# One ring block for both compressions' weights, and three modulation rides that change place, in a 4-layer hybrid attention stack

## The chip, the core and the metric

The kernel runs on one core of one Trainium2 chip. Its time is the device time of one launch in microseconds (us). The profile is of one execution of the same program.

## The reference, cut to what matters

A sequence of 512 tokens of width 1024 (float32) goes through an AB layer, a CD layer and then four adaptive layers, whose gains, shifts and gates come from a modulation vector. The change lies in the CD layer, in the output projection ahead of it, and in the first adaptive layer:

```python
def layer_ab(x, ...):
    ...
    return x + mix @ w_out                       # the output projection ahead of the CD layer

def nsa_compress(z, pe, w1, w2):                 # once for keys, once for values
    ...
    return jax.nn.silu(flat @ w1) @ w2           # w1: (32*64, 128)

def layer_cd(x, ...):
    y = rms_norm(x, norm_g) @ w_in
    qc, kc, vc, ks, vs, kw, vw, gc, zc, cq, ckv, kr, zd = split_cols(y, CD_SPLITS)
    ...

ml = ada_mods(c, ada_w[i], ada_b[i])             # a vector by a 1024 x 6144 matrix, 6 chunks of 1024
mc = ada_mods(c_ctx, ada_w[i], ada_b[i])
hl = modulate(rms_norm_2(x, norm1_g[i]), ml[0], ml[1])
yc, yl = gqa_mixer(hl, hc, ang, at_w_qkv[occ], ...)   # joint attention over x and context
```

## The kernel before, in words

The program is written by hand for each engine. Activations stay on the chip (`X`, `H` and an arena). All weights pass through a **ring of three slots** of 4096 floats for each of 128 partitions. A load fills one slot ("a block", up to 2 MB) and SyncE (SP) issues the loads in the order in which the blocks are used: L1305 waits until the block three places earlier is free, L1308 issues the load's pieces. Because SP works in order, a load also waits for all loads ahead of it. `freed_by` (L1182 on) says what frees a block: for a block of projection weights the last tile that reads it, for a modulation block the end of its sums on VectorE (DVE), for a compression block the `misc_pe` count after its matmuls.

A `project` stage is a list of groups `(block, tiles, ride)`. For each tile TensorE (PE) runs the matmuls (L1407), ScalarE (ACT) or DVE takes the result out of its bank, and `t.after` lists side steps that each engine does behind that tile: `mean` (L1436), `spread` (L1448) and `swap` (L1465) on PE, the reciprocal (L2418), the scaling (L2430) and the rotation (L2444, L2448) on DVE, the cosine product on GpSimd (POOL, L2790). A tile's bank is reused 3 or 6 tiles later.

A **ride** is one of the 12 modulation blocks of a layer (8 chunks of 128 rows by 512 columns). Behind the last tile of its group, DVE waits for its load and adds the 8 chunks up, scaled by the condition, into `partial` (L2292 and L2296, 16 operations where both x and the context need them). PE's part is a "modulation": 8 products with a column of ones, into bank 7 (L1367); it is done only when the next group ends (`ride` pops what is pending), and waits for DVE's sums. DVE then adds the bias (L2279).

```
            def ride(a):

                if pending:
                    modulation(pending.pop())
                if a:
                    pending.append(a)
```

The stages that matter: `residual_halves` for `ab_out` (4 groups of 4 tiles of 256 columns; the group with the ride is cut behind its second tile, L471 to L475); the CD projections (`cd_groups`, L748 to L771; tiles 0 to 41 are numbered in their order, `after(34, ...)` names the 34th); CD attention; `cd_out`; the norm; the three joint projections `at_qkv` (L999 to L1008); joint attention; `at_o`.

Order of the ring's blocks, from ab_out to at_o (m = a modulation block; the numbers are columns of cd_in):

```
ab_out0 m ab_out1 | 1024 m 0 m uq ukv m 2048 m m 512 m cmpK cmpV 1536 2464 m | cd_out0 m cd_out1 | at0 at1 at2 | at_o0 m at_o1
```

`cmpK` and `cmpV` are the first compression weights for keys and for values, 1 MB each in two pieces (two halves of the partitions). 1536 is the block of the gates `Z2[:, 1..4]` (tiles 34 to 37), 512 the block of tiles 30 to 33. PE's `compress` of keys (L1544) comes behind tile 34, that of values behind tile 35.

Of the kernel before, what the change touches and what calls it, by code (L numbers as in the profile page):

```python
# [27 lines left out]
HD = 64  # L28
# [8 lines left out]
CMP_STRIDE, CMP_LEN, CMP_HID = 16, 32, 128  # L37
CMP_HALF = CMP_LEN // 2
NCMP = S // CMP_STRIDE - 1
# [205 lines left out]
def build_program(nc, dram, out_dram, stages_kept=10000):  # L245
    ctx = ExitStack()
    with ctx:
# [3 lines left out]
        def sem(name):  # L251
            return ctx.enter_context(nc.semaphore(name))
# [31 lines left out]
        def bank(b, n=BANK, at=0):  # L284
            return psum[:, b * BANK + at:b * BANK + at + n]
# [46 lines left out]
        misc_pe, misc_act, misc_dve = sem("misc_pe"), sem("misc_act"), sem("misc_dve")  # L332
# [10 lines left out]
        def block(view, upper=None):  # L343


            shape = view.shape
            n = 1
            for d in shape[1:]:
                n *= d
            k = shape[1] if len(shape) == 3 else 1  # L350
            pieces = [(lambda x: x[0:shape[0]].rearrange("p (k n) -> p k n", k=k) if len(shape) == 3 else x[0:shape[0]], view)]
            if upper is not None:
                pieces.append((lambda x: x[HD:2 * HD].rearrange("p (k n) -> p k n", k=k), upper))
            return block_of(n, pieces)

        def block_of(n, pieces):


            assert n <= SLOT, n
            blocks.append((n, pieces))  # L360
            return len(blocks) - 1

        def columns(k, n, *pieces):


            return block_of(k * n, [(lambda x, c0=c0, c1=c0 + src.shape[1]: x.rearrange("p (k n) -> p k n", k=k)[:, :, c0:c1],
                                     src.rearrange("(k p) n -> p k n", p=P)) for c0, src in pieces])

        def slot(b, k):

            return ring[:, b % RING, 0:blocks[b][0]].rearrange("p (k n) -> p k n", k=k)
# [11 lines left out]
        def next_ada():  # L383

            if not ada_left:
                return None
            layer, j = ada_left.pop(0)
            b = block(dram["ada_w"][layer, :, 512 * j:512 * j + 512].rearrange("(k p) n -> p k n", p=P))
            return b, layer, j

        def stage(kind, **kw):
            kw["kind"] = kind
            kw.setdefault("loads", [])
            stages.append(kw)
            return kw
# [21 lines left out]
        def t_tile(b, k, col, width, act, n, taker, op, dst, arg=None, part=0, tile=None):  # L417

            w = slot(b, k)
            return Tile([(w[:, i, col:col + width], act[:, i, 0:n]) for i in range(k)],  # L420
                        (part, width, n), taker, op, dst, arg, tile)
# [26 lines left out]
        def residual_halves(src, op, arg, normed, rides=0, **kw):  # L448


            bs, groups = [], []
            for i in range(2):
                bs.append(block(src[:, BANK * i:BANK * i + BANK].rearrange("(k p) n -> p k n", p=P)))
                if i < rides:
                    groups.append(next_ada())
            rode = groups + [None] * (4 - len(groups))
            groups = []
            for h, cs in enumerate(halves):
                for i in range(2):
                    tiles = []  # L460
                    for j in range(4):
                        k = 4 * i + j
                        t = t_tile(bs[i], KD, P * j, P, H[:, :, cs], HALF, "dve", op, X[:, k, cs], arg(k))
                        t.part = h
                        t.after = normed.squares(h, [k])
                        normed.made[h, k] = t
                        tiles.append(t)
                    groups.append((bs[i], tiles, rode[2 * h + i]))
            groups[2][1][1].after.append(("nsum", normed, 0))
            groups[2][1][2].after.append(("nspread", normed, 0))  # L470
            sums_tile, parts = groups[3][1][2], []  # L471
            for b, tiles, a in groups:

                parts += [(b, tiles[0:2], a), (b, tiles[2:], None)] if a else [(b, tiles, None)]
            return stage("project", groups=parts, sums_tile=sums_tile, **kw)  # L475

        def second_half(tiles, normed, sum_at, spread_at):

# [48 lines left out]
        for c0 in range(0, 2560, 512):  # L527
            b = block(dram["ab_in"][:, IDX_COLS + c0:IDX_COLS + c0 + 512].rearrange("(k p) n -> p k n", p=P))
# [180 lines left out]
        cd_groups, cd_list, cmp_freed = [], [], {}  # L709

        def cd_block(c0, c1):
            return block(dram["cd_in"][:, c0:c1].rearrange("(k p) n -> p k n", p=P))

        def cd_group(b, tiles, rides=False):
            cd_groups.append((b, tiles, next_ada() if rides else None))
            cd_list.extend(tiles)


        b = cd_block(1024, 1536)
        lat_z = [("copy", CQ[:, 0]), ("copy", CQ[:, 1]), ("copy", CKV[:, 0]), ("silu", Z2[:, 0])]  # L720
        tiles = [t_tile(b, KD, P * j, P, H[:, :, cs], HALF, "act", op, dst[:, cs]) for cs in halves
                 for j, (op, dst) in enumerate(lat_z)]
# [5 lines left out]
        b = cd_block(0, 512)  # L728
        tiles = [t_tile(b, KD, P * j, P, H, S, "act", "copy", QC[:, j]) for j in range(4)]
# [3 lines left out]
        pieces = []  # L733
        for i in range(2):
# [3 lines left out]
            for q in range(2):  # L738
                for g in range(2):
# [3 lines left out]
        b = block_of(2 * 768, pieces)  # L743
        tiles = [t_tile(b, 2, P * t, P, CQ, S, "act", "copy", QU[:, t] if t < 4 else QR[:, t - 4]) for t in range(6)]
        cd_group(b, tiles)
        b = block(dram["ukv"])
        w = ring[:, b % RING, 0:1024]
        tiles = [Tile([(w[:, P * t:P * t + P], CKV[:, 0, :])], (0, P, S), "act", "copy", KU[:, t]) for t in range(4)]  # L748
        tiles += [Tile([(CKV[:, 0, tt * P:tt * P + P], w[:, 512:1024])], (0, P, 512), "act", "copy", VD[:, tt, :])
                  for tt in range(ST)]  # L750
        cd_group(b, tiles, True)
        b = columns(KD, 512, (0, dram["cd_in"][:, 2048:2432]),
                    *((384 + ROT * i, dram["cd_in"][:, 2432:2464]) for i in range(4)))
        cd_group(b, [t_tile(b, KD, 384, P, H, S, "act", "copy", KR[:, 0]),
# [1 line left out]
        cd_group(b, [t_tile(b, KD, P * j, P, H, S, "act", "silu", Z2[:, 5 + j]) for j in (1, 2)], True)  # L756
        b = cd_block(512, 1024)
        tiles = [t_tile(b, KD, P * j, P, H, S, "act", "copy", dst[:, 0]) for j, dst in enumerate((KC, VC, KS, KW))]
        cd_group(b, tiles, True)
        for kv in range(2):  # L760
            b = block(dram["cmp_w1"][kv, 0:CMP_HALF * HD].rearrange("(l d) m -> d l m", d=HD),
                      dram["cmp_w1"][kv, CMP_HALF * HD:].rearrange("(l d) m -> d l m", d=HD))
            cmp_freed[b] = (misc_pe, 3 + kv)
            cd_group(b, [])
        cmp_blocks = list(cmp_freed)
        b = cd_block(1536, 2048)
        tiles = [t_tile(b, KD, P * j, P, H, S, "act", "silu", Z2[:, 1 + j]) for j in range(4)]
        cd_group(b, tiles)
        b = cd_block(2464, 2744)
        cd_group(b, [n_tile(b, KD, 24, 256, H, tt, "act", "copy", VSW[:, tt, :]) for tt in range(ST)], True)  # L770
        cd_group(b, [n_tile(b, KD, 0, 24, H, tt, "act", "sigmoid", GC[:, tt, :]) for tt in range(ST)])  # L771
# [223 lines left out]
        at_groups, at_list = [], []  # L995
        for c0 in range(0, 1536, 512):
            b = block(dram["at_qkv"][:, c0:c0 + 512].rearrange("(k p) n -> p k n", p=P))
            if c0 < 1024:
                tiles = [t_tile(b, KD, P * j, P, H, S, "act", "copy", Q[:, c0 // P + j]) for j in range(4)]  # L999
                tiles += [t_tile(b, KD, P * j, P, CH, C, "act", "copy", QX[:, c0 // P + j]) for j in range(4)]  # L1000
            else:
                tiles = [t_tile(b, KD, P * j, P, H, S, "act", "copy", K2[:, j, 0:S]) for j in range(2)]
                tiles += [t_tile(b, KD, P * j, P, CH, C, "act", "copy", K2[:, j, S:S + C]) for j in range(2)]
                for tt in range(6):
                    src, t0 = (H, tt) if tt < ST else (CH, tt - ST)
                    tiles.append(n_tile(b, KD, 256, 256, src, t0, "act", "copy", V2[:, tt, :]))
            at_groups.append((b, tiles, None))
            at_list += tiles  # L1008
        at_rope = (rope_t[:, 2 * S:2 * S + P], rope_t[:, 0:S], rope_t[:, S:2 * S], work)
        for t0, count, is_x in ((0, 4, True), (4, 4, False), (8, 4, True), (12, 4, False), (16, 2, True), (18, 2, False)):  # L1010
# [336 lines left out]
        def _(pe):  # L1347
# [8 lines left out]
            def weights(b):  # L1356
                pe.wait_ge(weights_in[b % RING], landed[b])
# [179 lines left out]

            def compress(_, v):

                b1 = cmp_blocks[v]  # L1540
                weights(b1)
                open_bank(6 + v)
                for l in range(CMP_HALF):
                    last = nc.tensor.matmul(bank(6 + v, 2 * NCMP), slot(b1, CMP_HALF)[:, l, :],  # L1544
                                            cmp_in[v][:, 2 * NCMP * l:2 * NCMP * (l + 1)], start=(l == 0),
                                            stop=(l == CMP_HALF - 1))
                last.then_inc(misc_pe, 1)
                bank_freed[6 + v] = (misc_act, v + 1)
# [1341 lines left out]
```

## Time and profile before

| | |
|---|---|
| median of 3 runs | 4087.72 us (4080.39 to 4090.18) |
| the profiled execution | 4087.81 us |
| its span | 4085.7 us |
| granted TensorE clock, mean | 0.978 |
| busy: PE, DVE, ACT, POOL | 3926.6, 1751.1, 932.8, 506.3 us |
| HBM read | 334.01 MB, 83 GB/s over the span |

The profiled execution's time is 2.1 us above its span. Times in rows are us from the span's start. In a timeline, one row is a merged run of like instructions: start, us, engine, line, operation, output <- input, shapes, count, and in brackets the idle time before it and what ended it. PEclk 1.00 is the upper level of TensorE's clock (2.4 GHz), 0.50 the lower (1.2 GHz). CD attention runs from 661 to 824 us of the span.

### The profile page before, as it was taken

How to read it: one execution, taken by the hardware profiler on the slowest of the kernel's cores; microseconds unless marked ns; L12 is line 12 of the kernel's file. 1: busy time of each engine (PE TensorE's matmuls, PEld its weight loads, DVE VectorE, ACT ScalarE, POOL GpSimd, SP SyncE). 2: the span in 40 equal slices, each digit the busy share in tenths (PEclk: the TensorE clock that was granted, in tenths of full speed). 3: DMA queues.
4: the chain of work that ended last, by engine and by line, in shares of the span. 5: the costliest groups of instructions: out<-in, count | busy, mean ns of one | idle time of the engine just before them, and what ended most of it. 6: DMA issues, size and time to landing. Idle time of an engine off the chain costs nothing.

```text
span 4085.7 us, 42004 instructions
## 1 busy us (share of the span) xinstructions
PE 3926.6 (96%) x16600; PEld 2671.4 (65%) x16604; DVE 1751.1 (43%) x3123; ACT 932.8 (23%) x2131; POOL 506.3 (12%) x414
## 2 busy tenths in 40 slices
PE   9999979999999999999999899999999999999997
PEld 4458436545655565656545578888558888678886
DVE  2654444732673223111010555654675665224343
ACT  1141213621452211100010442020312111212020
POOL 1000000000000000000000421112432121111121
PEclk8999989999999999999999999999999999999999
DMA  3112332021002123223121314443202444112221
GB/s 125 62 42 84 116 98 79 1 74 41 24 1 61 62 82 107 100 99 108 62 72 64 86 30 154 165 167 103 83 21 83 165 165 144 67 62 83 83 83 42
DMA packets 226770, 342.38 MB, mean 84 GB/s; under 512 B 32209, under 2 KB 100209, under 8 KB 226545
## 3 DMA queue, kind: packets, MB, share of 16 engines
q1 hardware_dynamic: 202064, 322.44, 23.0%
q0 software_dynamic: 6816, 10.01, 1.2%
q10 hardware_dynamic: 17696, 7.26, 0.7%
q8 instruction: 134, 2.20, 0.2%
q14 instruction: 60, 0.48, 0.0%
HBM read 334.01 MB, written 4.06 MB: 83 GB/s over the span
## 4 chain that ended last, share of the span: by engine, by line
PE 73%; DVE 3%; POOL 1%; ACT 1%; issue 1%; DMA 0%; DVEq 0%; ACTq 0%; POOLq 0%
PE psum L1638 28%; PE psum L1407 28%; PE psum L1591 5%; PE psum L1595 3%; PE psum L1762 2%; PE psum L1709 2%; PE psum L1739 1%; PE psum L1507 1%; POOL arena L2774 1%; PE psum L1367 1%; DVE small L2594 1%; ACT arena L2079 1%; DVE psum L2590 0%; DVE arena L2609 0%; PE psum L1665 0%
## 5 line engine op out<-in xcount | busy, mean ns | idle before, releaser
L1407 PE MATMUL psum<-H,ring 128*128 128x512 f32 (+1 forms) x3248 | 1160.5, 517 | 38.1 <-DMA ring<-in_cd_in 22.8
L1407 PEld LDWEIGHTS psum<-H,ring 128*128 128x128 f32 x3248 | 622.0, 193 | 554.8 <-issue 483.9
L1638 PE MATMUL psum<-arena,ring 128*128 128x256 f32 x1536 | 342.8, 380 | 2.8 <-ACT arena L1876 2.8
L2296 DVE SCALAR_TENSOR_TENSOR arena<-ring,cond,arena 128x512 f32<-128x512 f32 x448 | 320.5, 754 | 8.0
L1638 PEld LDWEIGHTS psum<-arena,ring 128*128 128x128 f32 x1536 | 290.4, 190 | 44.0 <-ACT arena L1876 5.3
L2731 POOL TENSOR_TENSOR ring<-ring 128x1024 f32<-128x1024 f32 x48 | 159.6, 3325 | 791.0 <-DVE arena L2143 791.0
L1638 PE MATMUL psum<-arena 128*128 128x256 f32 x1152 | 256.3, 379 | 0.4
L1638 PEld LDWEIGHTS psum<-arena 128*128 128x128 f32 x1152 | 218.6, 190 | 30.3 <-ACT arena L1881 0.7
L2594 DVE TENSOR_REDUCE small<-psum 128x1 f32<-128x512 f32 (+7 forms) x352 | 187.0, 566 | 116.8 <-PE psum L1721 51.6
L2279 DVE TENSOR_TENSOR mods<-psum,vec 128x4 f32<-128x4 f32 (+1 forms) x48 | 7.7, 161 | 509.1 <-PE psum L1367 508.2
L1591 PE MATMUL psum<-arena,ring 128*128 128x512 f32 x512 | 225.6, 593 | 0.2 <-issue 0.2
L2067 ACT ACTIVATE arena<-psum,small 128x256 f32<-128x256 f32 (+7 forms) x320 | 183.8, 579 | 121.7 <-DVE small L2594 79.5
L1407 PE MATMUL psum<-CH,ring 128*128 128x256 f32 x928 | 206.7, 380 | 0.0
L1407 PEld LDWEIGHTS psum<-CH,ring 128*128 128x128 f32 x928 | 175.2, 190 | 39.9 <-issue 14.3
L1739 PE MATMUL psum<-ident,arena 128*128 128x128 f32 x984 | 153.3, 286 | 33.4 <-ACT arena L2079 21.6
L1638 PE MATMUL psum<-H,ring 128*128 128x256 f32 x768 | 177.0, 383 | 5.2 <-issue 4.5
L1638 PE MATMUL psum<-CX,arena 128*128 128x256 f32 x768 | 175.0, 382 | 5.8 <-DVE CX L2163 5.8
L1831 ACT ACTIVATE arena<-psum 128x512 f32<-128x512 f32 (+1 forms) x116 | 61.1, 528 | 494.9 <-PE psum L1407 490.9
L1638 PE MATMUL psum<-CH,ring 128*128 128x256 f32 x768 | 169.7, 379 | 0.0
L1591 PEld LDWEIGHTS psum<-arena,ring 128*128 128x128 f32 x512 | 96.7, 190 | 108.6 <-issue 107.4
L1638 PEld LDWEIGHTS psum<-CX,arena 128*128 128x128 f32 x768 | 146.9, 192 | 27.1 <-issue 6.9
L1638 PEld LDWEIGHTS psum<-H,ring 128*128 128x128 f32 x768 | 145.7, 192 | 25.5 <-issue 5.2
(230 smaller groups left out, 4612.2 us busy)
## 6 DMA issues: line engine op xcount, KB each, us to landing
ring<-in_mlp_w SPq DMA_DIRECT2D x64, 2048.0 KB, 8.8
ring<-in_ada_w SPq DMA_DIRECT2D x48, 2048.0 KB, 7.9
ring<-in_na_qkv SPq DMA_DIRECT2D x6, 2048.0 KB, 8.0
ring<-in_ab_in SPq DMA_DIRECT2D x5, 2048.0 KB, 8.2
ring<-in_cd_in SPq DMA_DIRECT2D x4, 2048.0 KB, 7.7
ring<-in_pw SPq DMA_DIRECT2D x8, 1024.0 KB, 6.8
ring<-in_at_qkv SPq DMA_DIRECT2D x3, 2048.0 KB, 7.8
ring<-in_ab_out SPq DMA_DIRECT2D x2, 2048.0 KB, 8.2
```

What stands on the lines that cost most here:

```text
L1407: last = nc.tensor.matmul(out, lhs, rhs, start=(k == 0), stop=(k == len(t.pairs) - 1))
L1591: last = nc.tensor.matmul(bank(m), w[:, k, P * m:P * m + P], hid[:, KD * kb + k, :], start=(kb == 0 and k == 0), stop=(kb == 3 and k == KD ...
L1595: last = nc.tensor.matmul(bank(4 + m // 2, C, C * (m % 2)), w[:, k, P * m:P * m + P], hidc[:, KD * kb + k, :], start=(kb == 0 and k == 0 a ...
L1638: last = nc.tensor.matmul(bank(at, HALF, HALF * m), w[:, i, P * m:P * m + P], x[:, i, :], start=(opens and m == 0 and i == 0), stop=(i == ...
L1709: last = nc.tensor.matmul(psum[:, at:at + k1 - k0], p["q"](g, qt * P, qt * P + P), p["k"](g, a * P + k0, a * P + k1), start=(m < 3), stop= ...
L1739: last = nc.tensor.transpose(psum[0:rows, c0:c0 + P], pair["probs"][g][:, k0:k0 + rows], ident[:, :])
L1762: last = nc.tensor.matmul(psum[HD * g:HD * g + HD, at + q0:at + q1], p["v"](g, of[0] if of else kt), chunk["turned"][0:p["krows"], kt, g, ...
L1831: nc.scalar.activation(t.dst, src, ACT.Copy).then_inc(act_took, 1)
L2067: nc.scalar.activation(pair["probs"][g][:, 0:nk + more], psum[:, off:off + nk + more], ACT.Exp, bias=small[:, c:c + 1], accum_out=small[:, ...
L2296: ins = nc.vector.scalar_tensor_tensor(partial[:, v, :], w[:, k, :], cond[:, k, v:v + 1], partial[:, v, :], ALU.mult, ALU.add)
L2594: nc.vector.tensor_reduce(small[:, c:c + 1], psum[:, off:off + nk], AX, ALU.max, negate=True).then_inc(negmax_ready, 1)
L2731: nc.gpsimd.tensor_tensor(a21, a11, a21, ALU.subtract).then_inc(s3_made, 1)
```

## The change

`residual_halves` no longer cuts the group with the ride: the ride comes behind the group's fourth tile, and PE's modulation one group later. In the CD projections, the groups of `ukv` and of block 512 carry no ride any more; `cmpK` and `cmpV` are one block of 4096 floats per partition in four pieces, freed by the fourth `misc_pe` (behind both compressions); the group of block 1536 is cut behind its first tile and carries a ride there. The second joint projection (`at_qkv` columns 512 to 1023) carries a ride. So six rides instead of seven lie in the CD projections and one in the joint projections; their number in all is the same. The ring's order becomes:

```
ab_out0 m ab_out1 | 1024 m 0 m uq ukv 2048 m m 512 cmp 1536 m 2464 m | cd_out0 m cd_out1 | at0 at1 m at2 | at_o0 m at_o1
```

```diff
-            sums_tile, parts = groups[3][1][2], []
-            for b, tiles, a in groups:
-
-                parts += [(b, tiles[0:2], a), (b, tiles[2:], None)] if a else [(b, tiles, None)]
-            return stage("project", groups=parts, sums_tile=sums_tile, **kw)
+            return stage("project", groups=groups, sums_tile=groups[3][1][2], **kw)
...
-        cd_group(b, tiles, True)
+        cd_group(b, tiles)
         b = columns(KD, 512, (0, dram["cd_in"][:, 2048:2432]),
...
-        cd_group(b, tiles, True)
+        cd_group(b, tiles)
+
+        pieces = []
         for kv in range(2):
-            b = block(dram["cmp_w1"][kv, 0:CMP_HALF * HD].rearrange("(l d) m -> d l m", d=HD),
-                      dram["cmp_w1"][kv, CMP_HALF * HD:].rearrange("(l d) m -> d l m", d=HD))
-            cmp_freed[b] = (misc_pe, 3 + kv)
-            cd_group(b, [])
-        cmp_blocks = list(cmp_freed)
+            for half in range(2):
+                pieces.append((lambda x, kv=kv, lo=HD * half: x[lo:lo + HD].rearrange(
+                                   "p (v l m) -> p v l m", v=2, m=CMP_HID)[:, kv],
+                               dram["cmp_w1"][kv, CMP_HALF * HD * half:CMP_HALF * HD * half + CMP_HALF * HD].rearrange(
+                                   "(l d) m -> d l m", d=HD)))
+        cmp_block = block_of(2 * CMP_HALF * CMP_HID, pieces)
+        cmp_freed[cmp_block] = (misc_pe, 4)
+        cd_group(cmp_block, [])
         b = cd_block(1536, 2048)
         tiles = [t_tile(b, KD, P * j, P, H, S, "act", "silu", Z2[:, 1 + j]) for j in range(4)]
-        cd_group(b, tiles)
+        cd_group(b, tiles[0:1], True)
+        cd_group(b, tiles[1:])
...
-            at_groups.append((b, tiles, None))
+            at_groups.append((b, tiles, next_ada() if c0 == 512 else None))
...
-                b1 = cmp_blocks[v]
-                weights(b1)
+                weights(cmp_block)
                 open_bank(6 + v)
                 for l in range(CMP_HALF):
-                    last = nc.tensor.matmul(bank(6 + v, 2 * NCMP), slot(b1, CMP_HALF)[:, l, :],
+                    last = nc.tensor.matmul(bank(6 + v, 2 * NCMP), slot(cmp_block, 2 * CMP_HALF)[:, CMP_HALF * v + l, :],
```

## Rows read from the trace of the kernel before

**Rows 1.** PE's waits over the span: us in total, times, longest us.
```profile
PE psum L1407 <- DMA ring<-in_cd_in: 22.8, 2, 18.0
...
PE psum L1367 <- DVE arena L2296: 4.1, 1, 4.1
```
**Rows 2.** Timeline of PE in ab_out.
```profile
320.87 14.05 PE L1407 MATMUL psum<-H,ring 128*128 128x256 f32 x64 [1.03 <-issue]
339.06 2.57 PE L1367 MATMUL psum<-ones,arena 128*128 128x1 f32 x16 [4.14 <-DVE arena L2296]
341.50 23.68 PE L1407 MATMUL psum<-H,ring 128*128 128x256 f32 x96
...
369.35 20.88 PE L1407 MATMUL psum<-H,ring 128*128 128x256 f32 x96
```
**Rows 3.** Timeline of DVE in ab_out.
```profile
329.18 9.83 DVE L2296 SCALAR_TENSOR_TENSOR arena<-ring,cond,arena 128x512 f32<-128x512 f32 x14
```
**Rows 4.** Stretch behind the first wait: us, busy by engine, PEclk, DMA, GB/s.
```profile
341.50:345.00 3.50, 3.50 (x9) 2.84 (x10) 0.17 (x1) 0.00 (x0) 0.00 (x0) 0.50 0.00 0
```
**Rows 5.** Timeline of PE in the CD projections.
```profile
502.35 1.95 PE L1367 MATMUL psum<-ones,arena 128*128 128x1 f32 x16
...
527.20 16.04 PE L1407 MATMUL psum<-H,ring 128*128 128x512 f32 x32 [4.87 <-DMA ring<-in_cd_in]
...
544.23 7.13 PE L1407 MATMUL psum<-H,ring 128*128 128x512 f32 x16
...
566.06 1.92 PE L1367 MATMUL psum<-ones,arena 128*128 128x1 f32 x16 [0.93 <-DVE arena L2444]
585.96 8.81 PE L1407 MATMUL psum<-H,ring 128*128 128x512 f32 x16 [17.98 <-DMA ring<-in_cd_in]
```
**Rows 6.** Timeline of SP in the CD projections: the issues of loads.
```profile
519.43 0.37 SPq L1308 DMA_DIRECT2D ring<-in_cd_in  x1
...
536.04 29.57 SPq L1308 DMA_DIRECT2D ring<-in_cmp_w  x4
578.28 21.61 SPq L1308 DMA_DIRECT2D ring<-in_cd_in  x2
```
**Rows 7.** Timeline of DVE: two modulation blocks' sums, and the reciprocal behind tile 34.
```profile
526.66 9.36 DVE L2296 SCALAR_TENSOR_TENSOR arena<-ring,cond,arena 128x512 f32<-128x512 f32 x14
...
568.90 9.36 DVE L2296 SCALAR_TENSOR_TENSOR arena<-ring,cond,arena 128x512 f32<-128x512 f32 x14
597.43 3.35 DVE L2418 RECIPROCAL arena<-arena 128x512 f32<-128x512 f32 x1 [19.18 <-ACT arena L1967]
```
**Rows 8.** DMA issues from 519 to 537: KB each, median us to landing.
```profile
ring<-in_cd_in SPq DMA_DIRECT2D x1, 2048.0 KB, 7.7
...
ring<-in_cmp_w SPq DMA_DIRECT2D x2, 512.0 KB, 6.2
```
**Rows 9.** Timeline of DVE in the joint projections.
```profile
1003.34 0.69 DVE L2448 TENSOR_TENSOR arena<-arena 128x512 f32<-128x512 f32 x1
1010.67 1.75 DVE L2418 RECIPROCAL arena<-arena 128x256 f32<-128x256 f32 x1 [6.64 <-ACT arena L1967]
```
**Rows 10.** Timeline of PE in the joint projections and behind them.
```profile
1016.55 0.70 PE L1448 MATMUL psum<-arena 64*128 64x256 f32 x4
...
1053.18 3.49 PE L1709 MATMUL psum<-arena 64*128 64x512 f32 x16 [0.67 <-ACTq L2111]
```
**Rows 11.** A stretch of CD attention; columns as in rows 4.
```profile
787.30:801.20 13.90, 13.90 (x75) 8.89 (x76) 5.33 (x27) 4.82 (x22) 0.00 (x0) 0.51 0.00 0
```
**Rows 12.** Timeline of PE in CD attention, third and fourth compressed branch.
```profile
757.65 0.41 PE L1709 MATMUL psum<-arena 64*128 64x31 f32 x4
...
773.65 0.65 PE L1762 MATMUL psum<-arena 31*64 31x256 f32 x4
...
783.97 0.41 PE L1709 MATMUL psum<-arena 64*128 64x31 f32 x4
...
805.52 0.65 PE L1762 MATMUL psum<-arena 31*64 31x256 f32 x4
```

## The prediction

> **What bounds the kernel now.** I read the page's busy times first, then PE's waits, then the timelines of PE, SP and DVE around the changed places, then the granted clock there. PE is busy for 3926.6 of the span's 4085.7 us, so only two things are to be had: time in which PE waits, and time in which it works at half clock. Of PE's waits two lines touch this change [rows 1]: one on loads of cd_in (22.8 us in two waits, the longest 18.0) and one of a modulation on DVE's sums (4.1 us). Rows 5 put the first pair at 522.3 (4.87 us, before block 512) and at 568.0 (17.98 us, before block 1536); rows 2 put the other at 334.9. In all three PE has nothing else to do, so they set the end.
>
> **Part 1, the ride in ab_out.** Now DVE sums behind the second tile and ends at 339.0 [rows 3]; PE has run tiles 0 to 3 by 334.9 (64 matmuls in 14.05 us, 3.5 us a tile), must do the modulation at once, and waits 4.14 us [rows 2]. The clock then is at its lower level [rows 4]: the modulation takes 2.57 us where another takes 1.92 [rows 5], and the next 96 matmuls take 23.68 where a later 96 take 20.88 [rows 2]. So the wait costs 4.14 + 0.65 + 2.80 = **7.6 us**. After the change DVE takes tile 3 at about 335.3 and sums for some 10.7 us (9.83 for the last 14 of 16 operations [rows 3]) until about 346.4; PE wants the modulation behind tile 7, at 334.9 + 4 x 3.46 = 348.7: 2.3 us to spare. Queued behind the sums on DVE are the takes of tiles 4 to 6; six banks are in turn, so PE needs the first of them only for tile 10, at about 357. The first half's norm needs tile 7, taken at about 349 either way. Gain 7.6 us; its bounds are 4.1 (if the clock falls anyway) and 7.6.
>
> **Part 2, the wait of 18 us.** (From here times are the old profile's, earlier gains not taken off.) Block 1536 is issued at 578.28, as DVE ends the sums that begin at 568.90 [rows 6, 7]: they free the block three places ahead, which rides with block 512. It is there 7.7 us later. In the new order the block three places ahead of 1536 is the second modulation block of group 2048, whose sums run at 526.66 to 536.0 [rows 7]. The load in front of it, cmp, waits for the sums before those, which begin behind the group's first half, at about 504, with the modulation of 502.35 [rows 5], and end 10.2 us later. So 1536 is issued at 536 instead of 578 and is there at 544, where PE wants it at 568. The wait of 17.98 us goes, and the half clock behind it: 8.81 us for a tile that takes 7.13 at full clock [rows 5], 1.7 us. Gain **19.7 us**; bounds 18.0 and 19.7. What is late next: nothing that I find. The four pieces of cmp go out behind block 512 at 519.8. One takes 6.2 us [rows 8]; even one behind the other they end at 544.6, where the first compression comes at about 576, and 1536 behind them is there at 552.
>
> **Part 3, the ride behind tile 34.** Its load needs block 512 free (564, where tile 33 ends) and lands by 572. On DVE it stands behind the reciprocal of tile 34's side steps. That ends 6.2 us behind tile 34 now (594.8 to 600.8 [rows 5, 7]), so at about 581 then, and the sums take 10.2 us (9.36 [rows 7] and 0.9 for the first two of the 16), to 591. Queued behind them is the scaling behind tile 36, at 598: 7 us to spare. The modulation comes behind tile 37 (606). Block 2464 waits for the second compression instead of the first: issued at 591, there by 599 even at a full block's 7.7 us [rows 8], wanted at about 612. The next ride waits for 1536 to be free (606), is there by 614, and DVE wants it at 624. All costed at nothing; without that cover PE would wait 3 to 10 us at a spread.
>
> **Part 4, a ride from the CD into the joint projections.** One modulation fewer between the halves of group 2048: the 1.95 us at 502.35 [rows 5], not hidden, since the next load is issued when that group ends. SP has one issue fewer there and one more ahead of at2; at2 now waits for at0's last tile, a whole group of tiles ahead of its use. In the joint projections DVE gets 10.2 us of sums from 1004.0 on [rows 9], to 1014.2; the reciprocal that ran at 1010.67 for 1.75 us then ends at 1016.0, and PE's spread wants it at 1016.55 [rows 10]: 0.6 us to spare, the narrowest margin of the change. A miss is bounded by 0 and about 3 us; I take 0, since the margin is positive. The new modulation comes behind the last tile, bare before attention [rows 10]: 1.9 us of PE. So part 4 is -1.95 + 1.9 = 0, with 0 to +3 as its bounds.
>
> **What stays.** The 4.87 us wait before block 512 and its slow first tile: that load still waits for the end of group 2048, at 519.43 [rows 6].
>
> **The sum.** 7.6 + 19.7 + 0 = 27.3 us less. The durations are of the profiled execution, 4087.81 us, 0.1 us from the median 4087.72: 4087.8 - 27.3 = **4060.5 us**.
>
> **Rival 1: the clock in CD attention falls elsewhere.** From 787.3 to 801.2 the granted clock is 0.51 although PE is busy all of it [rows 11]: a run of matmuls with few columns, in the fourth compressed branch. That branch takes 805.52 - 783.97 = 21.55 us to the point that the third, at full clock, reaches in 773.65 - 757.65 = 16.0 [rows 12]; one such fall costs 5.6 us, and I put 1.6 more for the slow stretch right behind it. The same work runs once at half clock and elsewhere at full, so it depends on more than the work, and the change moves this stage by 27 us. No fall: 4060.5 - 7.2 = 4053.3. Two more: 4060.5 + 11.2 = 4071.7. The Trainium skill (TensorE: Matmul & The Clock Gate, HAM oscillation — how this bites in real kernels) puts such falls on gaps in PE's work: by it the clock behind the two removed waits is won, as their rows bear out [rows 2, 5], and attention, unchanged, would stay as it is. Rows 11 show a fall without a gap, so I keep this rival.
>
> **Rival 2: block 1536 still comes late.** If something on the way through DVE, SP and the queue held it, the 18 us would stay in large part, and only part 1 is left: 4087.8 - 7.6 = 4080.2. The queue decides from the point where four pieces and the block behind them need over 48 us, that is 10.1 us a piece. For it: pieces of cmp are slow for their size [rows 8]. The Trainium skill speaks for it too (DMA: Bandwidth & Descriptors, Rules for kernel authors): transfers to two halves of the partitions serialize, and one over all 128 is wanted. By that the four would take the 24.8 us of part 2's bound, which still fits. Against: 24 us of margin.
>
> **Rival 3: DVE is late in the joint projections.** The reciprocal ends 3 us behind its need, and the half clock follows as in part 1 (3.5): 4060.5 + 6.5 = 4067.
>
> **Rival 4: slower than before.** The fall of the clock in rival 1 lasts. It cost 5.6 us in 13.9 us of low clock, 0.40 for each; CD attention runs over 163 us, and some 18 are low now. Low throughout it would lose 145 x 0.40 = 58 us: 4118.5. It decides from 27.3 / 0.40 = 68 us more of low clock on. For it: a fall without any wait [rows 11]. Against: the rest of the stage is at full clock now, as in the third branch [rows 12].
>
> **How the numbers follow.** Forecast 0.62, rival 1 0.24 (either way still faster), rival 2 0.05, rival 3 0.06, rival 4 0.03. The range reaches down to rival 1 with no fall and 1 us for the scatter, 4052, and up to two more falls, 4071, which holds rival 3 too; rivals 2 and 4 are left out. A measurement of this kernel can tell about 0.3%, 12 us, from no change: faster needs under 4075.5. Faster: 0.62 + 0.24 + 0.06 = 0.92. Within 0.3%: rival 2, 0.05. Slower: 0.03.
>
> **What would show it.** Among PE's waits the line on DVE L2296 is gone, and that on in_cd_in has one wait of about 4.9 us. SP issues the four of cmp_w together, right behind block 512, and 1536 some 16 us later. Tile 34 begins right behind a modulation and takes 7.1 us, not 8.8. A modulation stands between the last joint projection and attention. Compressed branches of 16.0 or of 21.6 us tell rival 1. A wait before tile 34, or before the spread that was at 1016.55, would prove a step wrong; a span less than 15 us shorter with those waits gone would prove the sum wrong.

## The result, and the profile after

The changed kernel takes 4065.0 us (median of 5 runs, 4058.48 to 4068.69), beside 4087.72 us for the kernel before in the same session (5 runs, 4080.39 to 4091.7): 22.7 us less, ratio 0.9943, 95% interval 0.9931 to 0.9956. The forecast was 4060.5 us, 27.3 less, with a range of 4052 to 4071. The profiled execution took 4068.68 us, 3.7 over its median; its span is 4066.6 us, 19.1 shorter.

PE's waits after the change. The columns are those of [rows 1]: us in total, times, longest.

```profile
span 4066.6 us, 42004 instructions
PE 3927.3 (97%) x16600; PEld 2669.9 (66%) x16604; DVE 1750.3 (43%) x3123; ACT 930.6 (23%) x2131; POOL 506.3 (12%) x414
...
PE psum L1409 <- DMA ring<-in_cd_in: 5.2, 1, 5.2
```

The wait of the modulation on DVE's sums has no line any more, and that on cd_in has one wait left of 5.2 us. In these two lines some 22 us of waiting are gone. PE's busy time, though, is 3927.3 us, where it was 3926.6. The forecast had put 5.2 us of half clock into the gain (0.65 + 2.80 behind the first wait, 1.7 behind the second); falls of the clock in other places, shown below, took as much back.

PE, around the changed places. These rows answer to [rows 2], [rows 5] and [rows 10].

```profile
324.39 27.86 PE L1409 MATMUL psum<-H,ring 128*128 128x256 f32 x128 [1.03 <-issue]
352.09 1.84 PE L1369 MATMUL psum<-ones,arena 128*128 128x1 f32 x16
...
523.13 17.04 PE L1409 MATMUL psum<-H,ring 128*128 128x512 f32 x32 [5.18 <-DMA ring<-in_cd_in]
...
562.99 1.92 PE L1369 MATMUL psum<-ones,arena 128*128 128x1 f32 x16 [0.93 <-DVE arena L2445]
564.77 7.11 PE L1409 MATMUL psum<-H,ring 128*128 128x512 f32 x16
...
1029.69 1.84 PE L1369 MATMUL psum<-ones,arena 128*128 128x1 f32 x16
1032.20 2.29 PE L1710 MATMUL psum<-arena 64*128 64x512 f32 x11 [0.66 <-issue]
```

The 128 matmuls of ab_out run through at full clock, and the modulation behind them does not wait. Tile 34 (564.77) follows its modulation without a wait and takes 7.11 us, where it waited 17.98 and took 8.81. The wait before block 512 (5.18) has stayed, with 17.04 us for its two tiles, 1.0 more than before. The last two rows are the new modulation between the joint projections and attention.

SP's issues, the answer to [rows 6], and the landings of the four pieces of cmp (KB each, median us).

```profile
515.04 0.37 SPq L1310 DMA_DIRECT2D ring<-in_cd_in  x1
515.46 9.84 SPq L1310 DMA_DIRECT2D ring<-in_cmp_w  x4
531.66 0.37 SPq L1310 DMA_DIRECT2D ring<-in_cd_in  x1
561.24 0.37 SPq L1310 DMA_DIRECT2D ring<-in_ada_w  x1
587.08 0.37 SPq L1310 DMA_DIRECT2D ring<-in_cd_in  x1
```
```profile
ring<-in_cmp_w SPq DMA_DIRECT2D x4, 512.0 KB, 10.6
```

Block 1536 is issued at 531.66 and there by 540, 25 us before it is wanted; before, that issue came at 578.28 and was the late one. From 523, behind block 512, to 532 the queue moves only the four pieces, at about 210 GB/s with the DMA engines fully busy, where blocks of cd_in move 400. The last piece landed at 532.8, that is 17.3 us after the first of them was issued (515.46); all of it was covered.

The joint projections, on DVE; these answer to [rows 9].

```profile
982.08 9.36 DVE L2297 SCALAR_TENSOR_TENSOR arena<-ring,cond,arena 128x512 f32<-128x512 f32 x14
991.36 1.74 DVE L2419 RECIPROCAL arena<-arena 128x256 f32<-128x256 f32 x1
```

The sums end, the reciprocal follows, and it ends at 993.1; PE's spread comes at 993.90 and does not wait. The margin was forecast as 0.6 us and is 0.8.

### The profile page after: what moved, and what is told of

It is laid out like the page before. It is cut to its first block, busy times and chain, and to the rows that moved or that the text cites. A ratio compares the mean times of both kernels' runs of the same rounds, so it can differ in the third digit from the quotient of the medians.

```text
span 4066.6 us, 42004 instructions
## 1 busy us (share of the span) xinstructions
PE 3927.3 (97%) x16600; PEld 2669.9 (66%) x16604; DVE 1750.3 (43%) x3123; ACT 930.6 (23%) x2131; POOL 506.3 (12%) x414
## 4 chain that ended last, share of the span: by engine, by line
PE 73%; DVE 3%; POOL 1%; ACT 1%; issue 1%; DMA 0%; ACTq 0%; DVEq 0%; POOLq 0%
PE psum L1639 29%; PE psum L1409 28%; PE psum L1592 5%; PE psum L1596 3%; PE psum L1763 2%; PE psum L1710 2%; PE psum L1740 1%; PE psum L1509 1%; PE psum L1369 1%; POOL arena L2775 1%; DVE small L2595 1%; ACT arena L2080 1%; DVE psum L2591 0%; DVE arena L2610 0%; PE psum L1666 0%
```

## The experiments

The theory: each removed wait is worth its length plus the half clock behind it, and the four parts add up; what is missing from 27.3 us lies in falls of the clock elsewhere. The rivals: a part of the change is worth less than its wait, or costs something that the forecast put at nothing. In the edits, "before" and "after" are the two kernels.

**Run 1: part 1 alone**, in the kernel before.

```diff
...
-                parts += [(b, tiles[0:2], a), (b, tiles[2:], None)] if a else [(b, tiles, None)]
-            return stage("project", groups=parts, sums_tile=sums_tile, **kw)
+            return stage("project", groups=groups, sums_tile=groups[3][1][2], **kw)
```

> Only the ride in ab_out is moved behind the fourth tile; all else as before. Theory (waits removed one by one, each worth its wait and the half clock behind it): 7.6 us less than before, PE's wait at L1367 on DVE's sums (4.14 us) gone, the 18 us before block 1536 unchanged. Rival (the time went elsewhere, the clock gives it back): 0 to 4 us less.

Measured: 4077.91 us (11 runs, 4073.54 to 4088.44), ratio 0.9984 [0.9974, 0.9995]. In its trace the stretch from ab_out's first matmul to the norm behind it is 7.76 us shorter, and it is 7.76 shorter in the changed kernel too. Part 1 is worth what the forecast said. (Between the medians are 9.9 us. In this trace CD attention is 1.5 us shorter than before's too, and what lies behind joint attention 3.3; the edit touches neither.)

**Run 2: the merged block alone**, and **run 3: the moved ride alone**, each in the kernel before.

```diff
...
+        cmp_block = block_of(2 * CMP_HALF * CMP_HID, pieces)
+        cmp_freed[cmp_block] = (misc_pe, 4)
+        cd_group(cmp_block, [])
...
```
```diff
-        cd_group(b, tiles, True)
+        cd_group(b, tiles)
...
-        cd_group(b, tiles)
+        cd_group(b, tiles[0:1], True)
+        cd_group(b, tiles[1:])
```

(Run 2 has the first, run 3 the second: the ride of block 512 goes behind tile 34.)

> Only the two compression blocks are merged; the ride stays with block 512. Block 1536 then waits for block 512 to be free (about 564) instead of for the sums of the ride (578): it lands at about 572 and PE, ready at 568, waits some 4 us instead of 18. Theory: 14 to 16 us less than before. Rival A (the merge does all of part 2): 19.7 less, no wait. Rival B (the merge alone does nothing): 0.

> Only the ride moves from block 512 to behind the first gate tile; the compression blocks stay two. Block 1536 is again three places behind block 512: issued at about 564, a wait of some 4 us instead of 18. Theory: 14 to 16 us less than before, the same as the merge alone. Rival A (the ride's place does all of part 2): 19.7 less. Rival B: 0.

Measured: run 2 4073.2 us (ratio 0.9962 [0.9948, 0.9976]), run 3 4072.34 us (0.9964 [0.9952, 0.9977]). First run 2's issues of loads on SP and PE's wait for block 1536, then the same two of run 3:

```profile
541.19 5.05 SPq L1313 DMA_DIRECT2D ring<-in_cmp_w  x4
569.45 14.35 SPq L1313 DMA_DIRECT2D ring<-in_cd_in  x2
...
578.29 10.05 PE L1412 MATMUL psum<-H,ring 128*128 128x512 f32 x16 [5.17 <-DMA ring<-in_cd_in]
```
```profile
566.34 0.37 SPq L1309 DMA_DIRECT2D ring<-in_cd_in  x1
...
574.75 8.58 PE L1408 MATMUL psum<-H,ring 128*128 128x512 f32 x16 [4.73 <-DMA ring<-in_cd_in]
```

Either half alone shortens the wait from 17.98 to about 5 us, and neither removes it. In run 2 the block three places ahead of 1536 is block 512 itself, in run 3 it is block 512 again, because the ride's block left the ring there: 1536 can then go out only when tile 33 is done, and needs over 8 us, in which PE has 3 us of work (a modulation with 0.9 us of waiting in front). Only both together put a block there that is free some 30 us before tile 33 is done (in the changed kernel 1536 is issued at 531.66, and the next load, which does wait for block 512, at 561.24). So each half alone is worth 12 to 13 us of wait and the second adds 5, whichever it is.

**Run 4: both halves of part 2**, without part 1 and without the ride in the joint projections.

> Merge and moved ride together, the ride at ukv kept, ab_out and the joint projections as before: part 2 alone. Theory: 19.7 us less than before, no wait before block 1536; the wait before block 512 stays at about 5 us. Rival (clock falls give a part back): 15 less or so, with more low clock elsewhere in the CD stages than before.

Measured: 4073.63 us (4070.01 to 4074.79), ratio 0.9965 [0.9952, 0.9978]. No wait is left before tile 34, as in the changed kernel, but the total is 14 us less and not 19.7. The granted clock says where the rest is (window, us, then busy time of PE, PEld, DVE, ACT and POOL, PEclk, DMA share, GB/s):

```profile
568.00:572.00 4.00, 4.00 (x7) 1.61 (x6) 0.00 (x0) 0.00 (x0) 0.00 (x0) 0.57 0.78 295
612.00:620.00 8.00, 8.00 (x31) 6.93 (x31) 0.51 (x2) 0.00 (x0) 0.00 (x0) 0.57 0.99 366
745.00:760.00 15.00, 15.00 (x85) 9.54 (x86) 6.00 (x30) 5.84 (x26) 0.00 (x0) 0.54 0.00 1
```

PE is busy in all of each, and the clock is at its lower level. The first two stand in the projections behind the removed wait and bring what part 2 is worth down to 18.1 us at the first compression and 15.6 at attention; the third is a fall in the third compressed branch. So the rival of the expectation holds, and the 19.7 of the theory do not arrive in the total. Runs 2 and 3, with 5 us of waiting more, had no fall in the branches and are as fast.

**Run 5: the changed kernel without the ride in the joint projections**; it stays behind `ukv`.

```diff
-        cd_group(b, tiles)
+        cd_group(b, tiles, True)
         b = columns(KD, 512, (0, dram["cd_in"][:, 2048:2432]),
...
-            at_groups.append((b, tiles, next_ada() if c0 == 512 else None))
+            at_groups.append((b, tiles, None))
```

> The changed kernel with the joint projections' ride put back behind ukv: parts 1 to 3 without part 4. Theory: the same time as the changed kernel (4065), since part 4 is -1.8 us between the halves of group 2048 and +1.7 before joint attention; seen from the start of ab_out, group 512 begins some 1.8 us later than in the changed kernel and joint attention at the same distance. Rival (DVE's sums in the joint projections cost PE a wait): 2 to 6 us faster than the changed kernel.

Measured: 4067.97 us (4065.95 to 4069.04), ratio 0.995 [0.9937, 0.9964]. It differs from the changed kernel by less than the two can be told apart, as a part 4 of about 0 wants; the rival, 2 to 6 us faster, did not come. In the trace the modulation is paid between the halves of group 2048 (1.8 us) and not before joint attention (1.8 us less there, and joint attention itself is 1.4 us shorter). Counted from ab_out's start, block 512 begins 3.5 us later than in the changed kernel and not 1.8: the clock falls once more here, from 501 us, where the changed kernel has no fall. Joint attention then begins 1.6 us further from ab_out's start, where the expectation had the same distance.

**Run 6: one more ride into the joint projections.** What stays of waits, the one before block 512, is there because a modulation block rides with group 2048's second half, so that 512 has group 2048 three places ahead. This version moves that ride behind the first joint projection. The ring's order is then `ukv 2048 m 512 cmp 1536 m 2464 m | ... | at0 m at1 m at2`.

```diff
-        cd_group(b, [t_tile(b, KD, P * j, P, H, S, "act", "silu", Z2[:, 5 + j]) for j in (1, 2)], True)
+        cd_group(b, [t_tile(b, KD, P * j, P, H, S, "act", "silu", Z2[:, 5 + j]) for j in (1, 2)])
...
-            at_groups.append((b, tiles, next_ada() if c0 == 512 else None))
+            at_groups.append((b, tiles, next_ada() if c0 < 1024 else None))
```

> The changed kernel with one more ride moved: that of group 2048's second half goes into the first joint projection. Block 512 then stands three places behind ukv instead of behind group 2048 itself, and is loaded at about 482 instead of 515. Theory: the last wait on a load in the CD projections goes (5.2 us, and 2.9 of half clock behind it), so does one modulation with its wait for bank 7 (2.8), and 1.8 come back as a modulation in the joint projections: 9.1 us less than the changed kernel, about 4056. Rival A: the wait only moves, before block 1536 or the compression (4061 to 4065). Rival B: the two rides in the joint projections make DVE late there: 4060 to 4070.

Measured: 4053.72 us (5 runs, 4053.31 to 4061.97), ratio 0.9922 [0.991, 0.9935].

**Runs 7 and 8: the changed kernel and the kernel before once more**, unchanged, one execution each.

> The changed kernel once more, unaltered, for its trace. If the falls of the clock belong to the kernel's own order of work, CD attention shows one fall, in the third compressed branch, and 20 us to 22 of low clock in the same places. If they hang on when the execution starts, they stand elsewhere or are missing, and the span is some 3 to 8 us off 4066.6.

> The kernel before once more, unaltered, for its trace. Same question as with the changed kernel: one fall of the clock in the fourth compressed branch of CD attention if it belongs to the kernel; another place, none or two if it hangs on when the execution starts. The waits of 4.1, 4.9 and 18.0 us are there in either case.

Measured: the changed kernel 4056.38 us (span 4054.4), the kernel before 4089.97 (span 4088.0). The same program is 12.2 us shorter than in its first profile, more than the 3 to 8 us that the expectation gave for falls that move. The kernel before has its waits of 4.1, 4.9 and 17.9 us again, and its fall in the fourth branch. Two stretches of CD attention (run 7 is 2 to 3.5 us ahead in them), first in the first profile of the changed kernel, then in run 7:

```profile
700.00:707.00 7.00, 6.83 (x29) 3.80 (x29) 2.63 (x9) 3.70 (x13) 0.00 (x0) 0.52 0.00 0
740.00:755.00 15.00, 15.00 (x84) 9.46 (x82) 5.99 (x30) 5.83 (x26) 0.00 (x0) 0.54 0.01 1
```
```profile
700.00:707.00 7.00, 7.00 (x46) 3.76 (x48) 4.07 (x13) 3.76 (x12) 0.00 (x0) 0.90 0.00 0
740.00:755.00 15.00, 13.74 (x104) 7.32 (x102) 11.97 (x46) 9.48 (x38) 0.00 (x0) 1.00 0.00 1
```

It is nearly the same run of instructions, once at 0.52 and 0.54, once at 0.90 and 1.00, with 84 matmuls done in the second window there and 104 here. Ahead of the fall stands one wait of 0.29 us (at 739.09, just behind the start of the branch); run 7 has the same wait of 0.29 us (735.63) and no fall behind it.

**Runs 9 and 10: the changed kernel and the version of run 6**, timed beside each other.

> The changed kernel again, timed beside the next one. Theory (the direct steps are fixed, the clock's falls are not): its times scatter between 4054.5 and 4069 as the two profiles so far (4066.6 and 4054.4 us of span) do, median about 4063, ratio to before 0.994. In its profile the landmark behind ab_out and the first compression stand where they stood, within 1 us, against ab_out's start (-7.8) and against tile 33 (-18 to -20); the compressed branches take 16.0 or 21.6 us each. Rival (4065.0 was a chip's offset): median within 1 us of 4065 minus or plus a common shift of before.

> The version with one more ride in the joint projections again. Direct steps against the changed kernel: the wait before block 512 (5.2 us) gone, the slow tiles behind it 17.04 to 13.98 (3.1 us), one modulation (1.8 us) moved from between the halves of group 2048 to behind the joint projections, 0 in sum: 8.2 us less, so a median near 4055 to 4057 where the changed kernel shows 4063 to 4065, ratio to before 0.992. Rival (the earlier 4053.7 was luck with the clock in attention): medians of the two equal within 2 us.

Measured: the changed kernel 4066.71 us (4056.35 to 4068.22, ratio 0.9939 [0.9926, 0.9953]), the version with two rides there 4053.42 us (4052.04 to 4054.86, ratio 0.9916 [0.9902, 0.9929]). The median forecast for the changed kernel, 4063, was missed by 3.7 us, its landmarks stood where expected; its fourth branch took 23.4 us, neither 16.0 nor 21.6. The medians are 13.3 us apart, so the rival of run 10's expectation, medians equal within 2 us, is out. Over both sessions the version has 9 times, 7 of them between 4052.0 and 4054.9; the changed kernel has 11, and none under 4056.3. PE in run 10 where the wait stood:

```profile
512.59 1.95 PE L1369 MATMUL psum<-ones,arena 128*128 128x1 f32 x16
514.40 13.98 PE L1409 MATMUL psum<-H,ring 128*128 128x512 f32 x32
```

No wait, and the two tiles take 13.98 us where they took 17.04. The direct steps came to 7.8 us for 8.2 expected, counted in the traces of runs 9 and 10: the wait 5.3, the slow tiles 3.1, and the modulation behind tile 33 with its wait 2.8, less 2.0 for a second modulation ahead of joint attention and 1.4 for lower clock in it. (The expectation had the place of the removed modulation wrong: the one between the halves of group 2048 was gone already.) Between the medians are 13.3 us, between the spans 14.4; of these 3.2 are there at the start of ab_out, where the two programs are the same, and 3.3 lie behind joint attention, where they are the same again. Both are the clock: low for longer near the start, and falling in two short stretches from 3109 and 3505 us in run 9, which run 10 has at full clock. First run 9, then run 10 at the same work:

```profile
26.00:44.00 18.00, 15.68 (x44) 9.08 (x45) 6.63 (x15) 2.45 (x7) 0.00 (x0) 0.62 0.30 92
3109.00:3113.00 4.00, 4.00 (x13) 3.20 (x12) 3.44 (x3) 1.63 (x4) 0.00 (x0) 0.57 0.01 2
3505.00:3509.00 4.00, 3.40 (x5) 1.58 (x6) 2.65 (x7) 3.25 (x8) 0.83 (x2) 0.57 1.04 402
```
```profile
26.00:44.00 18.00, 15.68 (x49) 7.98 (x49) 6.63 (x15) 3.68 (x9) 0.00 (x0) 0.81 0.29 91
3098.00:3102.00 4.00, 4.00 (x20) 3.54 (x19) 3.50 (x3) 2.11 (x5) 0.00 (x0) 1.00 0.01 2
3492.00:3496.00 4.00, 3.21 (x8) 1.57 (x9) 2.84 (x8) 3.91 (x10) 1.02 (x2) 1.00 1.04 404
```

Nothing in the version's edit accounts for these 6.5 us.

## Why the prediction was right, point by point

The same landmarks on PE in three profiles of the changed kernel (the first one, run 9, run 7), each as the shift against the kernel before that the stretch adds, in us. They are differences of start times of timeline rows.

| stretch | forecast | first | run 9 | run 7 |
|---|---|---|---|---|
| everything ahead of ab_out | 0 | +3.5 | +3.3 | -0.4 |
| ab_out (part 1) | -7.6 | -7.8 | -7.8 | -7.8 |
| norm, uq, ukv, up to the halves of 2048 | 0 | +1.6 | +1.6 | 0.0 |
| the modulation between the halves (part 4) | -1.95 | -1.5 | -1.3 | -1.5 |
| block 512: wait, its tiles | 0 | +1.0 | +0.8 | -0.6 |
| to the first compression (part 2) | -19.7 | -19.8 | -19.8 | -18.1 |
| rest of the CD projections (part 3) | 0 | -0.3 | -0.2 | +2.8 |
| CD attention | 0 | +1.4 | +0.4 | -5.2 |
| cd_out and norm | 0 | -1.0 | 0.0 | -1.0 |
| joint projections (part 4) | +1.9 | +1.8 | +1.7 | +0.2 |
| joint attention | 0 | +1.4 | +1.4 | +0.9 |
| the rest | 0 | +0.5 | +0.3 | -0.6 |
| span | -27.3 | -19.1 | -19.5 | -31.3 |

**Part 1 held**: 7.75 or 7.76 us in all seven profiles that have it (the first, and runs 1, 5, 6, 7, 9 and 10), for a forecast of 7.6 with 4.1 as its lower bound. The clock did come back with the wait, each time.

**Part 2 held**: 19.8 us for 19.7, but not in every execution. Of the seven profiles without the wait, three give 19.8 us (the first, runs 5 and 9), and runs 6 and 10, which lose a modulation here too, have tile 34 at full clock as well. In runs 4 and 7 part 2 gives 18.1, next to the lower bound of 18.0, because the clock falls at tile 34 although no wait for a load stands before it (the 0.93 us ahead of its modulation are there in every profile). Tile 34 in run 7:

```profile
557.62 8.81 PE L1409 MATMUL psum<-H,ring 128*128 128x512 f32 x16
```

The block three places ahead decided, as argued; the four pieces of cmp had landed after 17.3 us, within the bound of 24.8. Rival 2 is out. The rule cited from the Trainium skill (DMA: Bandwidth & Descriptors, Rules for kernel authors), that transfers to two halves of the partitions serialize, is neither shown nor refuted: the pieces ran at half the rate of a full block, but they also have rows of 512 bytes, and no run here separates the two.

**Part 3 held**: no spread waits for longer than before; PE's waits at spreads on the reciprocal are 2.7 us in three waits in the kernel before and in every run. (The 6.2 us that part 3 reads from 594.8 to 600.8 are 6.0; nothing hangs on it.)

**Part 4 was put at 0.** The two modulations nearly cancel (-1.5 and +1.8: the one taken out gives 1.8 us, of which 0.3 go into a longer wait before block 512), and the reciprocal had 0.8 us to spare where 0.6 were forecast; rival 3 is out. What the forecast had not costed comes behind the new modulation: joint attention begins with a low clock. First the changed kernel, then run 5 and the kernel before, which have no modulation there, each from about 4 us into joint attention:

```profile
1036.00:1046.00 10.00, 7.93 (x28) 5.15 (x28) 6.93 (x14) 6.42 (x13) 0.00 (x0) 0.66 0.25 64
```
```profile
1038.00:1048.00 10.00, 8.33 (x40) 5.62 (x40) 7.98 (x16) 7.11 (x16) 0.00 (x0) 0.83 0.35 98
1057.00:1067.00 10.00, 7.88 (x36) 5.19 (x36) 7.97 (x16) 7.18 (x15) 0.00 (x0) 0.83 0.44 136
```

Joint attention is 1.4 us longer than before's in the first profile and in run 9, 0.9 longer in run 7, as long as before's in runs 1 to 5 and 8, which have no modulation there, and 2.7 longer in runs 6 and 10 with two modulations in the joint projections. So part 4 costs 1.7 us in the first profile (-1.5, +1.8 and +1.4): within its bounds of 0 to 3, but for a reason that I had not seen.

**The step that was mis-sized is the clock outside the changed places**, that is the 0 in the sum for everything else. Two things are in it. The first is ahead of ab_out: in the first profile and in run 9 a stretch that no part of the change touches cost 3.5 and 3.3 us. (The same two profiles lose 1.6 us more in another short fall, from 451 us; run 7 has neither.) Kernel before, then the changed kernel:

```profile
26.00:44.00 18.00, 15.68 (x48) 7.99 (x48) 6.64 (x15) 3.69 (x9) 0.00 (x0) 0.81 0.30 93
```
```profile
26.00:44.00 18.00, 15.68 (x46) 9.08 (x46) 6.64 (x15) 2.45 (x7) 0.00 (x0) 0.62 0.30 92
```

The second is rival 1, with a forecast price of 5.6 us for a fall in a compressed branch. In the first profile the fall of [rows 11] moved from the fourth branch to the third (21.5 us to its last product; the fourth took 16.0), with a shorter one ahead of it. In run 7 there was none in the third and fourth, and CD attention was 5.2 us shorter. Where the branches are clean from start to end, as in runs 2 and 3, CD attention is 6.0 and 5.9 us shorter than before's (forecast for no fall: 7.2).

So the local steps, as the first profile has them, are 7.8 + 19.8 - 1.7 for part 4 - 1.0 for block 512 = 24.9 us, against 27.3 forecast and 22.7 between the medians: 2.4 us of the missing 4.6 are in steps costed at 0, and 2.2 are clock elsewhere. With the clock better than before's, as in run 7, the change is worth 31; with it as in the first profile, 19. Rival 1's two ends, 4053.3 and 4071.7, hold all 11 times of the changed kernel (4056.35 to 4068.69); so the range rested on the right cause, but only in part on the right place. Of the 5.8 us that the first profile loses outside the local steps, 1.4 are in CD attention, where rival 1 looked for them, and 5.1 ahead of the halves of group 2048 (the rows behind them bring 0.8 back): that the range held these too was luck. Rival 4, a lasting low clock, never showed: the longest fall in CD attention lasted some 20 us (run 9).

The rule of the Trainium skill cited there (TensorE: Matmul & The Clock Gate, HAM oscillation — how this bites in real kernels) puts falls on gaps in PE's work. At the two removed waits the first profile agrees: with the wait gone, the 128 matmuls of ab_out and tile 34 run at full clock. At tile 34 runs 4 and 7 do not: it took 8.81 us there with the wait gone. In attention the rule does not explain what is seen: PE is busy for 15.00 of 15.00 us at 0.54, and the same instructions ran at 1.00 in run 7.

**What stays open**: what decides in which compressed branch the clock falls, or whether it does. The kernel before fell in the fourth branch in both of its profiles (run 8: 789 to 803), the changed kernel in the third, in neither (run 7), and, in run 9, in the fourth (764 to 785, where that branch begins at 760.71); so it is not the program alone. Of the other runs 1, 5, 6 and 10 fell in the fourth, 4 in the third, 2 and 3 in none. Each of these long falls (14 or some 20 us) begins within 4 us behind the start of a branch. Whether the falls could be removed by other shapes of matmul in the branches was not tried. Why the version of run 6 keeps the better clock in nearly all of its executions, beyond its direct 7.8 us, is open too. And that the modulations cause the low clock in joint attention rests on three settings that agree (none in seven profiles: 0.0 us; one in three: 1.4, 1.4, 0.9; two in two: 2.7), not on a test that changes the clock alone.

## What to carry to other kernels

A load in a ring is late because of the block as many places ahead as the ring is deep: read which one that is before moving anything, since here either half of the edit only exchanged an 18 us wait for a 5 us one, and run 6 found the last one by the same rule. Cost a wait at its length plus the half clock behind it, with the length alone as the lower bound (both ends were seen here: 19.8 and 18.1 us for the wait of 18.0). Expect TensorE's clock to fall in other places too, also where PE has no gap: with these falls in other places, two executions of one program were 12 us apart here. So judge a change of 0.5% by local landmarks in the trace and by several timed executions, not by one span.

## What was not expected of the hardware

- Two executions of one program differ by 12.2 us in span with the same removed and kept waits (first profile and run 7), and the two of the kernel before by 2.3. The time at the lower clock level over the first 1400 us, added up from the granted clock, is 105.8 us in the first and 78.5 us in run 7.
- The clock is low with PE fully busy: 21.0 of 21.0 us at 0.51 in run 9.

```profile
764.00:785.00 21.00, 21.00 (x99) 11.36 (x98) 10.07 (x41) 8.34 (x35) 0.00 (x0) 0.51 0.00 1
```

- Eight products with a column of ones ahead of joint attention (1.84 us) are followed by 1.4 us lost to a lower clock (0.9 in run 7); with two such sets in the joint projections it is 2.7 us, with none 0.0.
- Four 512 KB pieces to half of the partitions each, in rows of 512 bytes, ran at about 210 GB/s together, a block of cd_in at 400.
